# A recurrent decoder step: the input chunks in three reduced passes, with the split made by ScalarE and GpSimd

## The reference, cut to what matters

```python
h = rmsnorm(x, p['norm_w'])
proj = einsum('bld,dn->bln', h, p['w_in'])          # 15 parts
y_s5  = s5_branch(...)          # complex diagonal recurrence
o_hg  = gated_chunk_scan(...)   # HGRN2; o_gla the same for GLA
o_ret = retention_chunk_scan(...)
mix = concatenate([y_s5 * silu(s5_z), y_hg * silu(hg_z), y_gla * silu(gla_z), y_ret * silu(ret_z)])
out = einsum('bln,nd->bld', mix, p['w_out'])
return x + out
```

## Time and profile before

| what | us |
|---|---|
| median of 3 runs | 356.77 |
| lowest, highest | 356.39, 358.14 |
| the profiled execution | 357.73 |
| its span, first to last instruction | 355.9 |
| TensorE busy / VectorE / ScalarE / GpSimd | 333.9 / 229.8 / 128.3 / 43.9 |

### The profile page before, as it was taken

One profiled execution on the slowest core, in us unless ns is written; L12 is line 12 of the kernel. 1 busy time (PEld: TensorE's weight loads), 2 busy tenths in 40 slices (PEclk: granted clock), 3 DMA queues, 4 the chain that ended last, 5 costly groups with the idle time before them and its releaser, 6 DMA issues.

```text
span 355.9 us, 6388 instructions
## 1 busy us (share of the span) xinstructions
PE 333.9 (94%) x2546; PEld 282.8 (79%) x2546; DVE 229.8 (65%) x481; ACT 128.3 (36%) x282; POOL 43.9 (12%) x81
## 2 busy tenths in 40 slices
PE   7899998889999999989979999999999999999991
PEld 6588876668889898769957888878888989767990
DVE  2574499986548973585559527596654897358454
ACT  4252001150780103982312620124276010596421
POOL 4028520006000002140000000000500000120000
PEclk9999999999999999899989999999999999989997
DMA  8977631232522401499805473322442433437503
GB/s 282 385 245 258 207 114 61 82 97 87 155 90 97 142 2 31 150 209 362 338 1 173 138 260 97 105 88 88 122 150 65 133 99 112 148 85 151 182 0 122
DMA packets 28012, 50.84 MB, mean 143 GB/s; under 512 B 6288, under 2 KB 6864, under 8 KB 27984
## 3 DMA queue, kind: packets, MB, share of 16 engines
q1 hardware_dynamic: 25968, 44.06, 37.3%
q0 software_dynamic: 1728, 6.29, 7.3%
q10 hardware_dynamic: 288, 0.09, 0.1%
HBM read 46.80 MB, written 3.64 MB: 142 GB/s over the span
## 4 chain that ended last, share of the span: by engine, by line
PE 68%; DVE 13%; ACT 10%; POOL 4%; issue 2%; DMA 1%; DVEq 0%; POOLq 0%; ACTq 0%
PE pr L486 39%; PE pr L759 10%; ACT u L966 4%; DVE att L1319 2%; PE wk L553 2%; DVE h L1051 2%; PE wk L675 2%; PE wk L500 2%; ACT w_lo L1027 2%; POOL lev L1556 2%; PE wk L598 1%; POOL lev L1558 1%; PE wk L566 1%; PE wk L667 1%; PE wk L613 1%
## 5 line engine op out<-in xcount | busy, mean ns | idle before, releaser
L486 PE MATMUL pr<-h,wring 128*128 128x264 f32 x768 | 184.2, 397 | 3.2 <-DVE h L1051 3.2
L486 PEld LDWEIGHTS pr<-h,wring 128*128 128x128 f32 x768 | 146.6, 194 | 31.5 <-issue 5.9
L759 PE MATMUL pr<-a_hi,w_hi 128*128 128x264 f32 x96 | 27.6, 288 | 0.0
L759 PE MATMUL pr<-a_lo,w_hi 128*128 128x264 f32 x96 | 27.2, 283 | 0.0
L759 PE MATMUL pr<-a_hi,w_lo 128*128 128x264 f32 x96 | 27.2, 283 | 0.0
L943 ACT ACTIVATE zs<-pr 128x264 f32<-128x264 f32 x16 | 6.0, 384 | 45.1 <-PE pr L486 45.0
L872 ACT ACTIVATE v<-pr 128x264 f32<-128x264 f32 x12 | 4.7, 388 | 48.2 <-PE pr L486 48.2
L860 ACT ACTIVATE h<-x 128x264 f32<-128x264 f32 x24 | 9.5, 420 | 32.7 <-DVE x L1460 30.6
L1319 DVE COPY_PREDICATED att<-masks,wk 128x512 f32<-128x512 int32 x20 | 17.6, 949 | 1.0
L759 PEld LDWEIGHTS pr<-a_hi,w_hi 128*128 128x128 f32 x96 | 18.1, 188 | 0.1
L759 PEld LDWEIGHTS pr<-a_lo,w_hi 128*128 128x128 f32 x96 | 18.1, 188 | 0.1
(11 more groups left out here) (279 smaller groups left out, 539.9 us busy)
## 6 DMA issues: line engine op xcount, KB each, us to landing
wring<-in_w_in SPq DMA_DIRECT2D x100, 256.0 KB, 3.0
wring<-in_w_out SPq DMA_DIRECT2D x20, 256.0 KB, 3.7
w_hi<-in_w_out POOLq DMA_DIRECT2D x6, 512.0 KB, 4.4
w_lo<-in_w_out POOLq DMA_DIRECT2D x6, 512.0 KB, 8.2
x<-in_xt SPq DMA_DIRECT2D x2, 528.0 KB, 4.6
out_y<-h SPq DMA_DIRECT2D x4, 264.0 KB, 2.1
s5m_t<-in_s5m SPq DMA_DIRECT2D x2, 512.0 KB, 4.9
ss<-in_hg_in SPq DMA_DIRECT2D x2, 512.0 KB, 4.0
```

Source lines behind the costliest of these rows:

```text
L486: mm = nc.tensor.matmul(ring_bank(layer, i)[:, 0:TT], wring[:, slot, n, :], act_in[:, k, :], start=(k == 0), stop=(k == KT - 1))
L759: mm = nc.tensor.matmul(ring_bank(layer, i)[:, 0:TT], w[:, j % WSLOTS, n, :], a[:, k, :], start=(k == 0 and p == 0), stop=(k == KT - 1 and ...
```

## The change

Input chunks 8 to 24 of layer 0 and 3 to 24 of layer 1 (`FIRST`) are done in three reduced passes, by the same function as the output chunks 2 to 7 (`product_of_parts`).

- The ring has 10 halves, and all chunks of both projections go through it; GpSimd's loads of output weights are gone. The high half goes to `w_hi` (4 halves, a tile of its own) for input chunks and to `o_hi` (6 halves, over `qh`) for output chunks. The low half is written in place over the ring's slot (`w_lo` over `wring`).
- ScalarE copies all high halves. For an input chunk it does so right after it has evacuated the second chunk before it (`next_high`). GpSimd subtracts for all low halves (`low_part`), in the order of the chunks, with its sample work placed between them.
- The normalized input is split as well: the high part `h_hi` lies over `x`, by ScalarE (`high_input`), the low part `h_lo` over the squares `sq`, by GpSimd (`low_input`). x is fetched back before the residuals: from the input in layer 0, in layer 1 from a copy in DRAM (`x_kept`) that SP writes while the first chunks run.
- `zs` is gone: silu writes into `h`. `qk` moves to `qm`. `s5_relay` is done in two parts, before and after chunk 17's silu. The load of S5's matrices for the next layer moves from output chunk 3 to 5.

```diff
...
-RING = 12
+RING = 10
+HRING = 4
+ORING = 6
+FIRST = (8, 3)
 PLAIN = 2
-BY_DMA = 3
-SPLIT = KT - PLAIN - BY_DMA
-RCH = NCH + KT - BY_DMA
-WSLOTS = 6
+CH = NCH + KT
+AHEAD = HRING // 2
...
-        zs = sb("zs", KT, TT)
+        w_hi = sb("w_hi", HRING, KH, P, dt=F32R)
+        sq = sb("sq", KT, TT)
...
+        qk = flat_qm[:, 1280:2048].rearrange("p (a t) -> p a t", a=3)
...
-        w_hi = over("w_hi", qh, WSLOTS, KH, P)
-        w_lo = over("w_lo", gates, WSLOTS, KH, P)
+        w_lo = over("w_lo", wring, RING, KH, P)
+        h_hi = over("h_hi", x, KT, TT)
+        h_lo = over("h_lo", sq, KT, TT)
+        o_hi = over("o_hi", qh, ORING, KH, P)
...
+        IN_SPLIT = [(layer, i) for layer in range(DEPTH) for i in range(FIRST[layer], NCH)]
+        def split_at(layer, i, half):
+            if i < NCH:
+                return 2 * IN_SPLIT.index((layer, i)) + half
+            return 2 * (layer * (KT - PLAIN) + i - NCH - PLAIN) + half
...
+            def chunk(layer, i):
+                src = w_in[layer, i] if i < NCH else w_out[layer, i - NCH]
+                for half in range(2):
+                    j = ring_at(layer, i, half)
+                    if j >= RING:
+                        before, last = divmod((j - RING) // 2, CH)
+                        half_done_by_pe(sp, before, last, half)
+                    sp.dma_start(wring[:, j % RING, :, :], src[:, KH * half:KH * half + KH]).then_inc(w_in_sem[j % RING], 16)
...
-                    chunk(w_in[layer, i])
+                    chunk(layer, i)
+                    if layer and i in (1, 4):
+                        n = i // 4
+                        sp.wait_ge(out_used, (layer - 1) * KT + KH * n + KH)
+                        part = slice(KH * n, KH * n + KH)
+                        sp.dma_start(x_kept[:, part, :], x[:, part, :]).then_inc(x_out, 16)
...
-                    if not PLAIN <= i < PLAIN + BY_DMA:
-                        chunk(w_out[layer, i])
+                    chunk(layer, NCH + i)
+                    if i == 4:
+                        sp.wait_ge(proj_done, layer * NCH + NCH)
+                        if layer:
+                            sp.wait_ge(x_out, 32 * layer)
+                        for n in range(2):
+                            part = slice(KH * n, KH * n + KH)
+                            sp.dma_start(x[:, part, :], (x_kept if layer else xt)[:, part, :]).then_inc(x_back[n], 16)
...
+            def product_of_parts(layer, i, done, hi, lo, hi_ready, lo_ready):
+                ring_free(pe, layer, i if i < NCH else i + 8)
+                bank = ring_bank(layer, i if i < NCH else i + 8)
+                for half in range(2):
+                    weight_hi, _, weights_ready, at = high_of(layer, i, half)
+                    weight_lo = w_lo[:, ring_at(layer, i, half) % RING, :, :]
+                    pe.wait_ge(weights_ready, at + 1)
+                    if hi_ready is not None:
+                        pe.wait_ge(hi_ready, layer * 2 + half + 1)
+                        pe.wait_ge(lo_ready, layer * 2 + half + 1)
+                    for n in range(KH):
+                        k = KH * half + n
+                        for p, (w, a) in enumerate(((weight_hi, hi), (weight_hi, lo), (weight_lo, hi))):
+                            mm = nc.tensor.matmul(bank[:, 0:TT], w[:, n, :], a[:, k, :],
+                                                  start=(k == 0 and p == 0), stop=(k == KT - 1 and p == 2))
+                    mm.then_inc(done if half else half_done, 1)
...
             def project(layer, i):
-                product(layer, i, proj_done, 2 * layer if i == 0 else None)
+                if i < FIRST[layer]:
+                    product(layer, i, proj_done, 2 * layer if i == 0 else None)
+                else:
+                    first = i == FIRST[layer]
+                    product_of_parts(layer, i, proj_done, h_hi, h_lo, hhi_ready if first else None, hlo_ready if first else None)
...
+            def high_part(layer, i):
+                for half in range(2):
+                    weights_in(act, layer, i, half)
+                    dst, ready, _, at = high_of(layer, i, half)
+                    if i < NCH and at >= HRING:
+                        half_done_by_pe(act, *IN_SPLIT[at // 2 - AHEAD], half)
+                    if i >= NCH:
+                        if i < NCH + PLAIN + ORING // 2:
+                            act.wait_ge(o_done, layer * 3 + 2)
+                        else:
+                            half_done_by_pe(act, layer, i - ORING // 2, half)
+                    step(fn(dst, wring[:, ring_at(layer, i, half) % RING, :, :], ACT.Copy), ready)
+            def high_input(layer, half):
+                act.wait_ge(h_ready, layer * KT + KH * half + KH)
+                if layer:
+                    act.wait_ge(x_out, 32 * layer)
+                part = slice(KH * half, KH * half + KH)
+                step(fn(h_hi[:, part, :], h[:, part, :], ACT.Copy), hhi_ready)
...
-                    if n and PLAIN <= k < KT - WSLOTS // 2:
-                        for j in (2 * (k - PLAIN) + WSLOTS, 2 * (k - PLAIN) + WSLOTS + 1):
-                            high_part(n - 1, j)
+                    step(fn(sq[:, k, :], x[:, k, :], ACT.Square), sq_ready)
+                    if n and PLAIN <= k < KT - ORING // 2:
+                        high_part(n - 1, NCH + k + ORING // 2)
                 act.wait_ge(ms_done, n + 1)
                 if n:
...
+                next_high(layer, i)
+            def next_high(layer, i):
+                if FIRST[layer] + (AHEAD if layer else 0) <= i + AHEAD < NCH:
+                    high_part(layer, i + AHEAD)
...
                     act.wait_ge(par_in, 16)
                     act.wait_ge(cst_in[0], 16)
                     lower_bounds()
+                else:
+                    for i in range(FIRST[layer], FIRST[layer] + AHEAD):
+                        high_part(layer, i)
+                for half in range(2):
+                    high_input(layer, half)
                 evac(layer, C_F0, x3[:, 0, :])
                 evac(layer, C_LR, lr_t)
                 evac(layer, C_F1, x3[:, 1, :])
                 use_silu()
                 turned(layer, 4, vt[:, :, 4:6, :])
                 evac(layer, C_U1, u[:, 1, :])
-                s5_relay(layer)
+                s5_relay(layer, range(0, 2))
...
                         step(fn(yt2, yt2, ACT.Tanh, scale=GELU_C), tanh_ready)
                         s5_back(layer)
                     silu(layer, i)
+                    if i == NP:
+                        s5_relay(layer, range(2, 4))
...
                         s5_turned(layer, range(4))
-                for n in range(BY_DMA):
-                    act.wait_ge(hi_in[n], 16 * (layer + 1))
-                    step(fn(w_lo[:, 2 * n:2 * n + 2, :, :], w_hi[:, 2 * n:2 * n + 2, :, :].bitcast(F32), ACT.Copy, scale=-1.0), neg_ready)
+                high_part(layer, NCH + PLAIN)
                 act.wait_ge(glu_done, layer + 1)
                 step(fn(glu[:, :, :], wk[:, 0:2, 0:TT], ACT.Tanh, scale=0.5), glu_tanh)
                 use_logs()
+                high_part(layer, NCH + PLAIN + 1)
                 for tiles in (range(0, 4), range(4, 6)):
...
                     part = rs[:, tiles.start:tiles.stop, :]
                     step(fn(part, part, ACT.Exp, scale=-0.5), ors_ready)
                 high_operand(layer)
+                high_part(layer, NCH + PLAIN + 2)
...
-            def low_part(layer, j):
-                dve.wait_ge(whi_ready, layer * 2 * SPLIT + j - 2 * BY_DMA + 1)
-                step(tt(w_lo[:, j % WSLOTS, :, :], wring[:, ring_slot(layer, j), :, :],
-                        w_hi[:, j % WSLOTS, :, :].bitcast(F32), ALU.subtract), wlo_ready)
+                    step(tt(a_lo[:, part, :], h[:, part, :], a_hi[:, part, :].bitcast(F32), ALU.subtract), alo_ready)
             def residual(layer, m):
+                if m % KH == 0:
+                    dve.wait_ge(x_back[m // KH], 16 * (layer + 1))
                 dve.wait_ge(out_done, layer * KT + m + 1)
...
                 low_operand(layer)
                 ret_states(layer)
                 for m in range(KT):
-                    if BY_DMA <= m < BY_DMA + SPLIT:
-                        low_part(layer, 2 * m)
-                        low_part(layer, 2 * m + 1)
...
-            def split_weights(layer):
-                pool.wait_ge(o_done, layer * 3 + 3)
-                for n in range(BY_DMA):
-                    part = w_hi[:, 2 * n:2 * n + 2, :, :].rearrange("p a k m -> p (a k m)")
-                    pool.dma_start(part, w_out[layer, PLAIN + n].rearrange("p k m -> p (k m)")).then_inc(hi_in[n], 16)
-                for n in range(BY_DMA):
-                    pool.wait_ge(neg_ready, layer * BY_DMA + n + 1)
-                    part = w_lo[:, 2 * n:2 * n + 2, :, :].rearrange("p a k m -> p (a k m)")
-                    pool.dma_start(part, w_out[layer, PLAIN + n].rearrange("p k m -> p (k m)"),
```

(37 more changed lines are left out.)

117 lines of the change are left out of this document (40 added, 77 removed).

## The result

The changed kernel takes 416.9 us (median of 4 runs, 415.5 to 418.7) where the kernel before takes 357.4: a ratio of 1.170, with a 95% interval of 1.165 to 1.174. The forecast was 369, at most 380. The direction was right, the size was not: the change costs 60 us, not 12. A few executions of a kernel show a lower granted clock and take longer than its others; the ratios leave them out.

The account below looks back on a forecast made before the run. Bound: layer 0 by a GpSimd and VectorE chain, layer 1 nearly throughout by TensorE. Layer 0 +11.2 and layer 1 +0.9 give +12.1 us on 356.77: 368.9, say 369; range 349 to 380.

Parts of the forecast that it names:

- What sets the end: VectorE and GpSimd chain in layer 0, mostly TensorE in layer 1, the scan with shorter chunks; GpSimd no bound.
- The saving of 0.68 us a chunk: TensorE, input chunks in three passes: 2.90 against 3.58 us each, 26.5 us for 39 chunks if nothing else waited.
- The turn: VectorE and GpSimd alternate by whole instructions: VectorE loses 0.8 us per low_part, bounded by 0.1 and 1.0.
- the share of 0.63: Layer 0, 40 to 72 us: 20 of VectorE's 32 us can collide with the twelve low_part instructions.
- Layer 0 up to the last level: Layer 0 to the last tree level: low_input turns 3.8 us, low_part 8 to 13 +5.5, together +9.3.
- The scan: S5 scan, each layer: it sets the end, 2.0 us of chunk savings lost, and low_part turns add +3.6.
- Layer 1 up to level 0: Layer 1 before level 0: at most 1.9 us gained, turns with scale_x, s5_c and the gate; +1.0 in all.
- rival (d): TensorE's clock halves after waits before s5_inputs and S5 outputs, up to four times: +7.6, 376.6 us; no separate chance.
- The tails by themselves: After the scan, each layer: chunk 23 saves 0.7, gates 0.5 later, restored x and high_part hidden; -0.2.
- (a): Flat toll on VectorE of 0.1 us per GpSimd instruction: total -7.5, 349 us; chance 0.22.
- (b): Nothing waits, the whole chunk saving stays: 356.8 - 26.5 = 330 us; chance 0.04.
- (c): GpSimd is the bound, 3.7 us a chunk against 2.90: up to 13 us more, 382; chance 0.08.

Follow-up runs that it names:

- e7: e1 also without ScalarE's 78 high_part copies of input chunks after the first four: groups at 345.4 and 346.4, 355.7 to 356.7, 366.0 to 368.6 us; profiled 356.3.
- e1: Changed kernel without GpSimd's low_part instructions, the third pass reading the high half again: 359.6 us, ratio 1.006.
- e8: Changed kernel with 37 idle 128x128 products on TensorE ahead of the wait for s5_outputs in each layer: 402.0 us, ratio 1.128.
- e3: Kernel before plus unused GpSimd subtractions where low_part and low_input of the input chunks stand: 418.1 us, ratio 1.170.

## Why the prediction was wrong, by its steps

- **What sets the end.** Right: VectorE's chain in layer 0, the scan, and GpSimd no bound. The saving of 0.68 us a chunk was right where TensorE sets the pace: the stretch from the turn of k to `s5_inputs` has seven such chunks and is 4.6 us shorter in both layers in e7. With ScalarE's copies, forecast at -1.5, it is -1.5 and -1.5 in e1, without the turns. With them it is +1.9 and +2.0; I had counted turns there as 0.2.
- **The price of low_part alone**: 1.15 taken, 1.26 measured (least of 78). Close.
- **The turn, the first step that failed.** That there is a turn was right; its size was not. The sum has 12 x 0.63 x 0.8 = 6.0 us for the twelve `low_part` of layer 0's levels, 0.5 each. Measured, from the end of the sines to the turn of k: 44.4 us against 31.9 before and 32.4 without `low_part` (e1), so 12.0, or 1.0 each. The bound of 1.0 was the right one and still low: VectorE loses 1.04 on an instruction of 80 elements and 1.08 on one of 16 (1.28 against 0.24, 1.25 against 0.17). And the share of 0.63 has no place here: the `low_part` come in rows of two to six, and nearly every one of them meets a VectorE instruction, however short. The first four met four of 0.8 us in all and made them 5.0.
- **Layer 0 up to the last level**: +9.3 said, +13.1 measured, +15.6 counted from `scale_x`. The sines started at 26.38, not 28, only because this execution began its work 2.5 us sooner: the input's turns cost 4.4 (`L1150` and `L1121`, 2.52 and 2.31 us for 0.24 and 0.20), 3.8 said. The series of sines itself was 1.2 shorter (14.2 against 15.5). The rest are the twelve turns behind it, above.
- **The scan**: +3.6 said, +7.1 measured. Four VectorE instructions under 7.65 us of GpSimd took 1.79, 2.20, 2.23 and 1.57 where before they took 0.68, 1.23, 1.20 and 0.69, and two more behind them 1.74 and 1.62 for 0.68 each: 6.0 together for six `low_part`, where the sum has 4.5 x 0.8. e1 has +2.5 and +1.3 without any turns, at the lower clock.
- **Layer 1 up to level 0**, the largest single error: +1.0 said, +8.0 measured (level 0 starts at 249.80, 39.9 us after `mean_square`, against 31.9 before). `s5_c`'s operations of 1280 elements, 1.49 us each before, were these:

```profile
218.20 3.50 DVE L1233 TENSOR_TENSOR ca_re<-are,s5m_t 128x1280 f32<-128x1280 f32 x1
221.62 3.71 DVE L1234 TENSOR_TENSOR qm<-aim,s5m_t 128x1280 f32<-128x1280 f32 x1
225.36 2.44 DVE L1236 TENSOR_TENSOR ca_re<-ca_re,qm 128x1280 f32<-128x1280 f32 x1
```

  I had let VectorE's wait of 2.16 us take half of the delay, and had left the gate's own sums out (`L1335`, four in 4.96 us, 1.11 before).
- **The clock, the second step that failed**, a term put at nothing: rival (d), "left out of the sum because nothing here shows how often". Of the 48 us between forecast and result, 18.8 lie in the two tails, and e8 shows 15 to 17 us for the two tails, where the rival had 7.6 for four waits. It priced a fall at 1.9 us, one chunk. A fall behind a wait is followed by the outputs, bound by TensorE throughout: in e7, 11.9 us.
- **The tails by themselves**: -0.2 said, +0.5 and +0.4 in e8. Right, with the restored x and `high_part` hidden as argued.
- **Rivals (a), (b), (c)** fell: no flat toll, the saving not there even without `low_part` (e1), GpSimd not the bound (5.6 us of TensorE's waits).

So of the 60 us, 15 to 17 are the tails' clock by e8, and e1 and e3 put the rest on the turns; it has other falls of the clock in it, which no run separates. From 40.6 to 85.0 us the granted clock is 0.81 on average (1.00 before), while VectorE is busy for 42.3 of the 44.4 us, so little of that stretch can be the clock's. In this window of layer 1's start it is 0.50:

```profile
216.00:221.00 5.00, 4.50 (x10) 3.20 (x10) 4.87 (x6) 2.17 (x2) 3.52 (x3) 0.50 0.15 54
```

## What to carry to other kernels

An idle GpSimd is no free engine beside a VectorE that sets the pace: price each GpSimd instruction that reads at its full length for the VectorE instruction that it meets, however short that one is, unless that takes its data from PSUM, and ask whether VectorE could do the work itself in less (0.69 us against 1.26 here). Spend a saving of TensorE only on the pieces where TensorE sets the pace: eight chunks placed so gave 1.1%, thirty-nine with their low halves on GpSimd cost 17%. And price a new wait of TensorE at more than its length, since what follows may run at half the clock.

## What the runs showed of the hardware that was not expected

- A wait of TensorE of 1.96 us was followed by a granted clock of 0.50 (1.2 GHz) in one layer and not in the other of the same execution (e7); the stages behind it took 68.7 and 57.5 us. After 0.34 us it was still 1.00 (2.4 GHz) in the window behind the wait, and the tails took 57.3 and 57.2 (e8). The three groups of e7 lie some 10 us apart; that this alone separates them is inferred.
- A VectorE TENSOR_SCALAR with one operand is held by GpSimd too: 0.20 became 2.31 us at 80 columns, 0.43 became 1.39 at 512. A copy from PSUM (`L1395`) under a `low_part` took 0.36, as before.
- GpSimd's subtraction takes 0.446 us at 128 columns and 1.26 at 512: the start of one costs about 0.18, and splitting it in four adds 0.5 us.
- GpSimd's memsets under VectorE's two-operand instructions cost VectorE nothing (0.24 and 0.17 us as before).
